# A weight ring and its upper parts with five places instead of six, in a two-block model on one core

## What is computed

```python
# first_block, two layers
x = x + 0.5 * swiglu(rmsnorm(x, g1), w_ffn1_in, w_ffn1_out)        # hidden width 2816
u = rmsnorm(x, g2)                                                  # u @ w_in -> three branches and their gates
x = x + (gates_0 * y_mla + gates_1 * y_hg + gates_2 * y_mem) @ w_out
x = x + 0.5 * swiglu(rmsnorm(x, g3), w_ffn2_in, w_ffn2_out)
# after both layers: rmsnorm(x, final_norm)
# second_block, two layers
x = layer_norm(ALPHA * x + 0.5 * swiglu(x, ffn1_w1, ffn1_w2))
x = layer_norm(ALPHA * x + token_mix(x, ...))     # compressed, selected, window, sink and forgetting attention
x = layer_norm(ALPHA * x + 0.5 * swiglu(x, ffn2_w1, ffn2_w2))
```

## Time and profile before

| | |
|---|---|
| median of 3 runs | 2603.3 us |
| the runs | 2603.73, 2603.30, 2597.07 us |
| the profiled execution's own time | 2598.8 us |
| its span | 2596.9 us |
| granted TensorE clock | 0.999 |
| busy: PE, POOL, ACT, VectorE (DVE) | 98%, 78%, 50%, 34% |
| ring loads | 862 of 512 KB, median 3.4 us from issue to landing |

### The profile page before, as it was taken

One profiled execution on the slowest core, in us unless ns is written; L12 is line 12 of the kernel. 1 busy time (PEld: TensorE's weight loads), 2 busy tenths in 40 slices (PEclk: granted clock), 3 DMA queues, 4 the chain that ended last, 5 costly groups with the idle time before them and its releaser, 6 DMA issues.

```text
span 2596.9 us, 48520 instructions
## 1 busy us (share of the span) xinstructions
PE 2556.8 (98%) x19862; PEld 2356.3 (91%) x19862; DVE 879.0 (34%) x1518; ACT 1287.1 (50%) x1934; POOL 2031.4 (78%) x906
## 2 busy tenths in 40 slices
PE   7999999999999999999999999999999999999998
PEld 6999999899899989989989998998998999899897
DVE  2744364211233436411121133833122132474212
ACT  4545565444444555544444445755444444574443
POOL 7988666898898856688888886478888888547886
PEclk9999999999999999999999999999999999999999
DMA  6566544555656654655665556245556556535554
GB/s 236 188 204 202 188 138 132 196 193 188 211 187 199 205 186 138 168 198 187 193 200 188 185 187 219 91 168 193 191 182 206 193 179 195 195 99 179 196 192 140
DMA packets 128739, 474.81 MB, mean 183 GB/s; under 512 B 14432, under 2 KB 14432, under 8 KB 127520
## 3 DMA queue, kind: packets, MB, share of 16 engines
q1 hardware_dynamic: 124704, 454.09, 53.0%
q0 software_dynamic: 3840, 17.83, 2.4%
HBM read 469.24 MB, written 2.62 MB: 182 GB/s over the span
## 4 chain that ended last, share of the span: by engine, by line
PE 91%; DVE 5%; ACT 2%; DMA 1%; issue 1%; POOL 1%; DVEq 0%; SPq 0%; ACTq 0%; POOLq 0%
PE psA L385 51%; PE psY L385 38%; PE psT L436 2%; DMA ring<-in_weights 1%; DVE psY L1285 0%; POOL rest L1071 0%; ACT upper L1882 0%; DVE psY L1273 0%; PE psT L660 0%; DMA cst<-in_consts 0%; DVE st L1370 0%; DVE x L1300 0%; ACT xT_upper L1882 0%; ACT G L1913 0%; DVE Sc L1345 0%
## 5 line engine op out<-in xcount | busy, mean ns | idle before, releaser
L1071 POOL TENSOR_TENSOR rest<-ring,upper 128x1024 fp32r<-128x1024 f32 (+1 forms) x834 | 1991.8, 2409 | 499.7 <-ACT upper L1882 490.1
L1882 ACT ACTIVATE upper<-ring 128x1024 fp32r<-128x1024 f32 (+1 forms) x834 | 870.2, 1053 | 755.2 <-DMA ring<-in_weights 754.2
L385 PE MATMUL psA<-xT_upper,upper 128*128 128x256 f32 x2784 | 381.3, 280 | 0.6 <-ACT arena L1882 0.6
L385 PE MATMUL psA<-xT_rest,upper 128*128 128x256 f32 x2784 | 377.5, 278 | 0.0
L385 PE MATMUL psA<-xT_upper,rest 128*128 128x256 f32 x2784 | 377.5, 278 | 0.0
L1326 DVE TENSOR_TENSOR psA<-sil,psA 128x256 f32<-128x256 f32 x144 | 61.8, 429 | 917.9 <-ACT sil L1882 917.7
L385 PEld LDWEIGHTS psA<-xT_upper,upper 128*128 128x128 f32 x2784 | 351.3, 188 | 4.3 <-ACT arena L1882 1.3
L385 PEld LDWEIGHTS psA<-xT_rest,upper 128*128 128x128 f32 x2784 | 346.3, 188 | 0.0
L385 PEld LDWEIGHTS psA<-xT_upper,rest 128*128 128x128 f32 x2784 | 346.3, 188 | 0.0
L385 PE MATMUL psY<-upper,hT_upper 128*128 128x512 f32 x704 | 201.6, 391 | 1.1 <-DVE hT_rest L1328 1.1
L385 PE MATMUL psY<-upper,hT_rest 128*128 128x512 f32 x704 | 200.5, 390 | 0.0
(11 more groups left out here) (282 smaller groups left out, 3042.1 us busy)
## 6 DMA issues: line engine op xcount, KB each, us to landing
ring<-in_weights SPq DMA_DIRECT2D x862, 512.0 KB, 3.4
G<-in_rows POOLq DMA_DIRECT2D x6, 1024.0 KB, 6.4
G<-in_rows POOLq DMA_DIRECT2D x7, 512.0 KB, 6.4
arena<-rel_by_distance POOLq DMA_DIRECT2D x8, 256.0 KB, 7.5
x<-in_x SPq DMA_DIRECT2D x2, 512.0 KB, 5.9
par<-in_params POOLq DMA_DIRECT2D x4, 256.0 KB, 5.7
xn<-in_mem POOLq DMA_DIRECT2D x1, 1024.0 KB, 9.3
memory_transposed<-arena POOLq DMA_DIRECT2D x1, 1024.0 KB, 5.3
```

What stands on the lines that cost most here:

```text
L385: i = pe.matmul(out, lhsT, rhs, start=start, stop=stop)
L1071: pool.tensor_tensor(rest[:, r, 0:n], ring[:, r, 0:n], upper[:, r, 0:n], ALU.subtract)\
L1882: act.activation(out, in_, func, **kw).then_inc(*up)
```

## The change

```diff
--- before.py
+++ after.py
@@ -35,7 +35,7 @@
 LOW = -1.0e29
 
 PIECE = 1024
-R = 6
+R = 5
 PIECES = (218, 213)
 LAYERS = 2 * DEPTH
 ALL_PIECES = DEPTH * sum(PIECES)
```

## The result

The changed kernel takes 2655.5 us (median of 4 runs, 2647.3 to 2661.7), the kernel before 2603.3: a ratio of 1.0214 (1.0199 to 1.0228). That is 52 us more. The profiled execution took 2657.0 us against 2598.8, which is 58.2 more, where the sum had 26.6 us. 2655.5 lies above the range, which ended at 2652.

The account below looks back on a forecast made before the run. PE, busy 2556.8 of 2596.9 us, was taken as the bound. Terms of 9.8, 13.0 and 3.8 us summed to 26.6, giving 2625.4 from the profiled execution or 2629.9 from the median; forecast 2628, range 2610 to 2652.

Parts of the forecast that it names:

- What bounds the kernel now: Whole kernel: PE is nearly always busy; one place less delays each load by one piece, free inside the long runs.
- Term 1: Seven feed-forward ends: the last silu waits behind N0's split; 2 x 2.0 + 5 x 1.15 = 9.8 us.
- room: Hidden tiles other than each feed-forward's last: PE wants them about 8 us after they are summed, so no stall.
- Term 2: Boundaries from a tail into by_halves: N2 and N3 are issued later; 4 x 2.0 + 5 x 1.0 = 13.0 us.
- The part with `uppers(norm, 0)` behind N2: Boundaries: ACT's three `uppers` (1.15 us) run only after N2's copy, putting N3's copy behind them.
- no second stall: RMS boundaries: second-half squares and POOL's pow come later by as much as PE does, so nothing more was counted.
- backlog rival: Boundaries and compression stages: POOL falls behind, a third pass waits too, 3.5 us at 11 places, 38 in all: 2664; chance 0.14.
- Term 3: Two compression stages, where PE runs at the loads' heels: each load moves one issue later, 1.9 us each, 3.8 us.
- At no cost: The start, the first block's raw pieces, attention, SP's shorter loop and the freed 8 KB: priced at nothing.
- Hidden: Rival: the sixth place is spare everywhere, stalls only where a weight piece itself is late, 5 us: 2604; chance 0.08.
- Faster: Rival: the new layout makes all 256-column matmuls run at the quick pace, saving 17.5 us: 2586; chance 0.04.
- The signs: Expected: late silu, by_halves' fourth pair waiting 1 to 2 us, `ACT upper` and `DVE hT_rest` waits about 10, pitch unchanged.

Follow-up runs that it names:

- e7: Four places of everything, where the changed kernel has five: 2821.8 us (single run).
- e3: Changed kernel, with each feed-forward's last silu no longer behind the split of the next stage's first piece: 2639.5 us, ratio 1.0137 to the kernel before.
- e4: Changed kernel, with ACT rounding the transposed residual ahead of N2's split at each norm's boundary: 2658.9 us, ratio 1.0241 to the kernel before.
- e1: Changed kernel, with VectorE scaling the residual before its wait for the parameters instead of behind it: 2640.4 us, ratio 1.0155 to the kernel before.
- e10: Changed kernel with six places of upper, still five of ring and rest: 2655.2 us, ratio 1.0204 to the kernel before.
- e5: Kernel before (six places), with GpSimd issuing the parameters' load one subtraction later in the second block: 2608.1 us, ratio 1.0032 to the kernel before.
- e6: Changed kernel with six places of ring and rest, five of upper, and one more ACT wait ahead of a copy: 2600.6 us, ratio 1.0002 to the kernel before.
- e12: Seven places of ring and rest, five of upper, against six of each in the kernel before: 2601.3 us, ratio 1.0002.
- e11: Six places of ring and rest, four of upper, against six of each in the kernel before: 2644.9 us, ratio 1.0169.
- e13: The changed kernel unaltered, run once more for comparison with e14 on one chip: 2657.5 us, ratio 1.0223 to the kernel before.
- e14: The kernel of e8 again, on the same chip as e13: 2652.2 us, ratio 1.0205 to the kernel before.
- e8: Changed kernel, with PE running matmuls nobody reads ahead of feed-forwards' last hidden tiles and the second block's wait for DVE O: 2651.7 us.

## Why the prediction was wrong

**The direction, the places and the mechanism of its terms held.** *What bounds the kernel now*: a place less delays each load by one piece, and in the long runs this costs nothing. POOL's and ACT's rows show the same durations as before, and e7's long runs nearly hold even with four places. The price sits at the boundaries.

**Term 1, the end of a feed-forward: 9.8 us, measured 10.4** at the seven ends: PE waits there for 2.74, 1.07, 0.85, 1.97, 0.79, 1.98 and 2.03 us, 11.4 in all, 1.07 of which it waited before. The mechanism is confirmed by the rows and by e3 at six of them. The first, where DVE was late already (1.1 us in the earlier trace rows), cost 1.67 more and didn't answer to e3. Two more waits for hT_rest, 1.8 us, stand at hidden tiles that are not the last of their feed-forward; these had "room", which failed there.

**Term 2, from a tail into by_halves: 13.0 us, measured about 15**: 6.2 under `issue`, 3.9 for `ACT upper` ahead of by_halves and 5.0 for DVE xn. Two steps of it failed. The part with `uppers(norm, 0)` behind N2 is real but no price of its own (e4). And "the pow on POOL ... come later by as much as PE does, so I count no second stall" is wrong: DVE xn appears with 5.0 us. One of its two places, in the timelines of POOL and PE:

```profile
1134.10 4.76 POOL L1071 TENSOR_TENSOR rest<-ring,upper 128x1024 fp32r<-128x1024 f32 x2 [2.13 <-ACT upper L1882]
1138.82 0.57 POOL L1051 TENSOR_TENSOR st<-st,cst 128x1 f32<-128x1 f32 x1
...
1140.31 1.78 PE L436 MATMUL psT<-cst,xn 128*128 128x128 f32 x8 [1.96 <-DVE xn L1261]
```

POOL's pow stood behind two subtractions of pieces that had landed late. That is the backlog rival's mechanism at two places, not at eleven.

**Term 3, the compression stage: 3.8 us, measured 4.9**, by how much PE's matmuls slip against the trace before between the first raw piece and the last gate piece: 1.8 and 3.1 us. The two stages were priced alike, at 1.9 each.

All of PE's new idle time but the 8.4 us for DVE O is 33.2 us, where the sum had 26.6: inside the upper bound of 45. It includes 1.6 us for DVE arena L1624, ahead of raw pieces of the first block, which stood under "At no cost".

**"At no cost" was the step that failed first.** It went through SP's loop, raw pieces, attention and the freed memory, and put at nothing, without naming it, what POOL issues besides subtractions. `load_params` stands behind `upto(5)`, and N5 now waits for N0 to be given back. The row for the parameters' wait was there before, on DVE, as a 10 us idle time that cost nothing. With the scaling held up behind it, it now cost 8.4 us of PE's idle time, and 15 us in all (e1).

**And each stall was priced at its own length**, with PE's busy time left as it was. The trace before had no stretch at half clock while PE worked, and two waits of over 2 us without one behind them, so it gave no hint. After, there are 30.7 us of them and 16.6 us more of busy time. A forecast that turned "PE waits" into "PE waits, then often works at half speed for a while" would have added about 13 us. I had named "PE's busy time itself moves by 10 us" as a sign of being wrong, but for another reason (pace).

With both: 26.6 + 8.4 + 16.6 = 51.6; the remaining 6.6 of 58.2 us are the terms that came out larger and small waits that no term had.

**The rivals.** *Hidden* (2604) is out: no order of instructions brought it back, and six places of upper alone don't either (e10). *Backlog* (2664) gave a total near the result for the wrong reason: PE's waits for `POOL rest` are 2.9 us after (1.7 and 1.2), against 2.6 before. *Faster*: the pitch of the 256-column matmuls, worked out from their starts, was 115.5 ns on average before and 115.4 after (outside the half-clock stretches), so the new layout changed no pace.

**The signs.** As announced: the late silu, `hT_rest` from 1 to 13, ACT's ring wait up, pitch unchanged. Off: the fourth pair in by_halves waits at four of the ten only (0.3 to 1.8 us; at five the first matmul waits), `ACT upper` rose to 9.1 rather than 10, and PE's busy time moved by 16.6 us without a change of pace.

## What to carry to other kernels

When a buffer's depth changes, follow not only the consumers of its pieces but everything that stands behind their `upto` on each queue, small DMA issues above all, and ask for each at whose busy stretch the late result will arrive. Size the stages of a buffer apart: the depth that counts is the one that hides the longest latency (here a landing of 3.4 us behind stages that hold three and four places at once, which needs the sixth place; the long runs do without it), and the copies behind it can have fewer (five cost nothing, four 42 us). And price a new stall on a saturated PE above its own length: here 41.6 us of waits brought some 12 us of slow work between typical runs, and 16.6 between the two profiled ones.

## What the runs showed of the hardware

- A 128x2048 float32 scaling in SBUF takes 1.22 us on VectorE alone, and 7.5 to 10.6 us in 19 cases in which it became ready while GpSimd worked through a row of subtractions (8.69 in the change, 7.54 in e5, 10.55 in e7). In each of these it runs when the last subtraction of the row ends, three or four ends after it became ready, though POOL pauses for 0.5 us in some of these rows to issue a load. In the kernel before, e6 and e12 it became ready 0.07 to 0.45 us before a subtraction's end and ran at that end (1.23 to 1.54 us in all; the next subtraction took 3.4 or 3.5 instead of 2.4), and once in e4 it took 3.4, where GpSimd's row ended with the subtraction in progress. In e10, e11, e3, e13 and e14 it was ready 0.06 to 0.21 us before one and was passed over. What decides it stays open. The form with an accumulator takes 2.28 us in both cases.
- Small work is held up too: a subtraction of 128x4 numbers on VectorE, both inputs in SBUF, took 16.01 us and ended with GpSimd's eight subtractions in a row (e12); it took 0.93 to 6.8 us in the other runs.
- TensorE's granted clock falls to its low level, 1.2 GHz, for 3.4 or 6.8 us at a time, in or behind waits of PE such as the 1.97 and 4.14 us above, but not behind each: seven of eleven waits of 1.9 us or more in the changed kernel. The same kernel differs from run to run: 0.991 to 0.995 in the changed kernel's nine runs, 2647 to 2665 us. With six places it was 0.996 to 0.999. A comparison within 0.3% needs several runs for that reason alone. The Trainium skill, "TensorE: Matmul & The Clock Gate", section "HAM oscillation — how this bites in real kernels", describes such falls behind idle time of PE, in a kernel that waits 3 to 5 us for its loads; the traces agree that falls follow waits, and have them behind waits of 2 us too, and e8 and e14 lean the same way.
- A single landing of 512 KB in a burst of loads took from 3.3 to 5.5 us (N3 in e4), where the earlier trace rows had 4.35.
